# First projection columns taken by input rows, adaLN units moved, overflow list made at the end of expert 0

## The reference

```python
cond = silu(c)
for l in range(2):
    mod = cond @ ada_w[l] + ada_b[l]              # 6 x 1024: shift, scale, gate, twice
    sh_m, sc_m, g_m, sh_f, sc_f, g_f = split(mod, 6)
    h = rms_norm(x, mix_pre_g[l]) * (1 + sc_m) + sh_m
    z = h @ w_in[l]                                # 7696 columns
    y_a = conv branch(z): a*sigmoid(g), causal depthwise conv of 31 taps,
          layer norm, silu, @ w_conv_out
    y_b = stick-breaking attention of 8 heads @ w_sb_out
    y_c = gated linear attention of 4 heads (16 low-rank columns give its decay)
          @ w_gla_out
    y = (g_a*y_a + g_b*y_b + g_c*y_c) @ w_o        # sigmoid gates from z
    x = x + g_m * rms_norm(y, mix_post_g[l])
    h = rms_norm(x, ffn_pre_g[l]) * (1 + sc_f) + sh_f
    y = swiglu(h) if l == 0 else moe_swiglu(h)     # dense 2816; top 2 of 8 experts, 3584
    x = x + g_f * rms_norm(y, ffn_post_g[l])
```

## Time and profile before

| what | us |
|---|---|
| median of 3 runs | 1854.64 |
| lowest and highest | 1853.37 and 1854.91 |
| the profiled execution | 1851.58 |
| its span, first to last instruction | 1849.7 |
| TensorE matmul busy in the span | 1782.7 (96%) |
| VectorE busy | 1533.6 (83%) |
| ScalarE busy | 1133.5 (61%) |
| mean granted TensorE clock | 0.989 |

### The profile page before, as it was taken

How to read it: one execution, slowest core, us unless ns; L and a number is a source line. 1 busy time by engine, 2 the same in 40 slices (tenths; PEclk the granted TensorE clock), 3 DMA queues, 4 the chain that set the end, 5 groups by cost and what they waited for, 6 DMA issues and landing times.

```text
span 1849.7 us, 28685 instructions
## 1 busy us (share of the span) xinstructions
PE 1782.7 (96%) x10843; PEld 1577.2 (85%) x10844; DVE 1533.6 (83%) x1422; ACT 1133.5 (61%) x954; POOL 193.6 (10%) x159
## 2 busy tenths in 40 slices
PE   2999999999999999989999999999999999999997
PEld 2999999899979999978888888888888888888886
DVE  6998866999657667767889898898898988988986
ACT  3444564533354554656777777767777777677774
POOL 0396001000006900000000000000000000000000
PEclk7999999999999999999999999999999999999999
DMA  9865534699735333444999989989999899899992
GB/s 381 356 239 200 175 138 163 229 392 362 260 108 185 135 137 137 160 153 181 364 355 363 373 330 375 366 338 363 353 361 372 330 376 370 335 366 348 361 374 94
DMA packets 72521, 525.30 MB, mean 284 GB/s; under 512 B 8112, under 2 KB 8240, under 8 KB 8704
## 3 DMA queue, kind: packets, MB, share of 16 engines
q1 hardware_dynamic: 72288, 524.03, 74.6%
q0 software_dynamic: 160, 0.23, 0.0%
HBM read 523.17 MB, written 1.05 MB: 283 GB/s over the span
## 4 chain that ended last, share of the span: by engine, by line
PE 55%; DVE 2%; ACT 0%; issue 0%; DVEq 0%; ACTq 0%
PE bank L1654 33%; PE bank L1669 16%; PE bank L1689 2%; PE bank L1679 1%; PE bank L1381 1%; PE bank L1352 1%; PE bank L1709 0%; PE bank L1710 0%; DVE arena L943 0%; DVE arena L947 0%; PE bank L1619 0%; DVE arena L1066 0%; PE bank L1626 0%; DVE w_lo L878 0%; DVE arena L1058 0%
## 5 line engine op out<-in xcount | busy, mean ns | idle before, releaser
L1127 DVE TENSOR_TENSOR w_lo<-raw,w_hi 128x2048 fp32r<-128x2048 f32 x224 | 510.0, 2291 | 82.9 <-ACT w_hi L752 82.9
L752 ACT ACTIVATE w_hi<-raw 128x2048 fp32r<-128x2048 f32 x224 | 428.5, 1916 | 97.0 <-PE bank L1669 70.4
L1381 PE MATMUL bank<-acts,w_hi 128*128 128x256 f32 x2080 | 374.2, 284 | 27.7 <-DVE acts L933 21.1
L1381 PEld LDWEIGHTS bank<-acts,w_hi 128*128 128x128 f32 x2080 | 321.4, 191 | 33.1 <-issue 24.6
L1654 PE MATMUL bank<-acts 128*128 128x512 f32 x1248 | 304.3, 392 | 2.5 <-DVE acts L1127 2.5
L1654 PE MATMUL bank<-w_hi,acts 128*128 128x512 f32 x960 | 297.3, 391 | 0.0
L1381 PE MATMUL bank<-acts,w_lo 128*128 128x256 f32 x1040 | 292.6, 281 | 0.0
L1654 PEld LDWEIGHTS bank<-acts 128*128 128x128 f32 x1248 | 231.3, 188 | 49.3 <-DVE acts L1127 2.9
L1127 DVE TENSOR_TENSOR acts<-raw,acts 128x2048 fp32r<-128x2048 f32 x112 | 256.1, 2287 | 19.9 <-ACT acts L752 19.9
L752 ACT ACTIVATE acts<-raw 128x2048 fp32r<-128x2048 f32 x112 | 215.1, 1921 | 72.2 <-PE bank L1654 69.8
L1669 PE MATMUL bank<-w_hi,acts 128*128 128x512 f32 x832 | 256.1, 389 | 0.0
(11 more groups left out here) (234 smaller groups left out, 2120.7 us busy)
## 6 DMA issues: line engine op xcount, KB each, us to landing
raw<-in_experts SPq DMA_DIRECT2D x336, 1024.0 KB, 5.1
raw<-in_stream SPq DMA_DIRECT2D x161, 1024.0 KB, 6.3
arena<-in_x_t SPq DMA_DIRECT2D x1, 1024.0 KB, 11.8
out_t<-arena SPq DMA_DIRECT2D x2, 512.0 KB, 2.6
arena<-in_c_row SPq DMA_DIRECT2D x1, 512.0 KB, 4.7
arena<-in_vecs SPq DMA_DIRECT2D x1, 224.0 KB, 2.5
arena<-in_glr_w POOLq DMA_DIRECT2D x2, 64.0 KB, 4.2
arena<-in_a POOLq DMA_DIRECT2D x2, 32.0 KB, 4.5
```

The source lines that it names most:

```text
L752: act.activation(expert_hi[s], raw[:, slot, :], ACT.Copy).then_inc(hi_written, 1)
L1127: dve.tensor_tensor(expert_lo[s], raw[:, slot, :], f32(expert_hi[s]), ALU.subtract).then_inc(raw_taken, 1)
L1381: mm = pe.matmul(out[:, c, :], w[:, 256 * k + P * c:256 * k + P * c + P], (hi if high else lo)[:, k, :], start=(k == 0 and n == 0 and c == 0),
```

## The change

Four things are done together.

1. The first eight columns of layer 0's input projection (`FIRST`) come by input rows. A unit `("zk", 0, k, 0)` holds 128 rows of w_in, those of chunk k, by the 2048 columns of z 0 to 7. The stream begins ada 0, zk 0, ada 1, zk 1, and so on. As soon as ada k is taken, VectorE finishes chunk k of shift and scale, scales chunk k, takes the low part of zk k and splits the chunk; `project_rows` multiplies it into all eight banks at once. x is loaded first, in halves; five products on constants stand ahead of TensorE's first sums. The evacuation of the eight columns, the two `glu` and the low-rank product follow when all rows are in; conv taps of layer 0 run in the iterations 9 to 25, and on VectorE and GpSimd they wait for the low-rank product, which reads the same memory.
2. Of layer 0's other 16 adaLN units, five stand behind z columns 9, 11, 13, 15, 17, three behind 26, 27, 28, four behind the units of "wo", and four go first in the feed-forward. Units of g = 2 are laid out so that the first four hold the scale and the last four the gate.
3. `finish_mods` becomes four functions, each called where its values are first needed; `ADA_TURN` goes from (3, 6, 9) to (5, 7, 10).
4. `list_overflow` is called behind the last tile of expert 0.

```diff
+FIRST = 8
+ADA_AFTER = (9, 11, 13, 15, 17, 26, 27, 28)
 def plan():
-    units = [("ada", 0, 0, k) for k in range(KC)]
+    units = []
+    for k in range(KC):
+        units += [("ada", 0, 0, k), ("zk", 0, k, 0)]
     for layer in range(DEPTH):
-        later = [("ada", 0, g, k) for g in (1, 2) for k in range(KC)] if layer == 0 else []
-        for u in range(Z_UNITS + G_UNITS):
+        later = [("ada", 0, 1, k) for k in range(KC)] + [("ada", 0, 2, k) for k in range(4)]
+        for u in range(FIRST if layer == 0 else 0, Z_UNITS + G_UNITS):
             units.append(("z", layer, u, 0))
-            if later and (u < 9 or u % 2):
+            if layer == 0 and u in ADA_AFTER:
                 units.append(later.pop(0))
         units += [("out", layer, b, h) for b in (1, 0, 2) for h in range(2)]
-        units += [("wo", layer, q, 0) for q in range(4)]
+        for q in range(4):
+            units.append(("wo", layer, q, 0))
+            if layer == 0 and later:
+                units.append(later.pop(0))
         if layer == 0:
-            later = [("ada", 1, g, k) for g in range(3) for k in range(KC)]
+            later = [("ada", 0, 2, k) for k in range(4, KC)]
+            later += [("ada", 1, g, k) for g in range(3) for k in range(KC)]
...
 # SyncE
+            for half in range(2):
+                c = KC // 2 * half
+                sp.dma_start(x[:, c:c + KC // 2, :], x_t[:, c:c + KC // 2, :]).then_inc(x_loaded[half], 16)
+            sp.dma_start(cond[0], c_row.to_broadcast([P, D])).then_inc(cond_loaded, 16)
             sp.dma_start(ar[:, C_VEC:C_VEC + N_VEC], vecs).then_inc(vec_loaded, 16)
-            sp.dma_start(cond[0], c_row.to_broadcast([P, D])).then_inc(cond_loaded, 16)
             for n in range(RAW):
                 sp.dma_start(raw[:, n, :], stream[n]).then_inc(loaded[n], 16)
-                if n == 1:
-                    sp.dma_start(x, x_t).then_inc(x_loaded, 16)
...
 # GpSimd
                 wait_read(pool, ("z", layer, 3, 0))
+                pool.wait_ge(lr_ready, layer + 1)
                 taps(layer, 0, TAPS)
...
 # ScalarE
+            act.preload_act_table(ACT.Silu)
+            act.wait_ge(consts, 5)
+            square_x(0)
             act.wait_ge(cond_loaded, 16)
             act.activation(cond[0], cond[0], ACT.Silu).then_inc(cond_ready, 1)
             root_ahead()
-            act.wait_ge(consts, 5)
-            act.wait_ge(x_loaded, 16)
-            norm_x(0)
+            norm()
+            act.wait_ge(vec_loaded, 16)
+            write_hi(("zk", 0, 0, 0))
+            for k in range(KC):
+                shift_chunk(0, SH_M, 1, k)
+                if k + 1 < KC:
+                    write_hi(("zk", 0, k + 1, 0))
...
 # VectorE
+            dve.wait_ge(vec_loaded, 16)
+            for k in range(KC):
+                add_ada(next(order))
+                if k == 0:
+                    inverse_root()
+                finish_mixer_in(0, k)
+                scale_chunk(0, A_M, k)
+                take(("zk", 0, k, 0))
+                split_chunk(1, k)
...
-                        first = (4, 4, 6)[c]
+                        first = (4, 4, 6)[c] if layer else FIRST + 1
...
-                if layer == 0 and i == 12:
-                    finish_mods(0, 1)
-                if layer == 0 and i == 24:
-                    finish_mods(0, 2)
...
                         if i == 1:
+                            finish_mixer_out(0)
+                            finish_ffn_in(0)
                             mixer_out(layer)
...
                 add_result(step)
-                if first:
-                    list_overflow()
...
                         tile(step, r, q * 2, q * 2 + (1 + r), True)
+                if first:
+                    list_overflow()
                 column = column_of(step + 1)
                 select(column, sel, chosen_f, sel_ready)
...
 # TensorE
+            def project_rows(k):
+                u = ("zk", 0, k, 0)
+                pe.wait_ge(raw_taken, POS[u] + 1)
+                pe.wait_ge(h_split, k + 1)
+                s = SLOT[u]
+                for c in range(2 * FIRST):
+                    out = two(bank[c // 2])[:, c % 2, :]
+                    for n, (w, high) in enumerate(parts(s)):
+                        mm = pe.matmul(out, w[:, P * c:P * c + P], (h_hi if high else h_lo)[:, k, :],
+                                       start=(k == 0 and n == 0 and c % 2 == 0),
+                                       stop=(k == KC - 1 and n == 2), skip_group_check=True)
+                    if k == KC - 1 and c % 2 and c < 2 * FIRST - 1:
+                        mm.then_inc(columns_done, 1)
+                mm.then_inc(consumed, 1)
...
-                if i == 0:
+                if i == (0 if layer else FIRST):
+                    if layer == 0:
+                        wait_read(pe, ("z", layer, 7, 0))
                     low_rank(layer)
...
+            for _ in range(5):
+                pe.matmul(bank[0][:, :], ones, area(C_ID, 4 * P), start=True, stop=True)
             norm_sums()
+            pe.wait_ge(norm_root, 1)
+            for k in range(KC):
+                project_rows(k)
```

More of the change, by code:

```diff
@@ L102, in plan, with ada_groups @@
     return units
+def ada_groups(g, k):
+    if g == 2:
+        return [16 * g + 8 * (k // 4) + 2 * (k % 4) + j for j in range(2)]
+    return [16 * g + 8 * j + k for j in range(2)]
 PLAN = plan()
@@ L109 @@
 POS = {u: n for n, u in enumerate(PLAN)}
+ADA_EARLY = [u for u in PLAN if u[0] == "ada" and POS[u] < POS["z", 0, 27, 0]]
 WPOS = {u: n for n, u in enumerate(W_UNITS)}
@@ L373, in mixer_units @@
         def mixer_units(layer):
-            return [u for u in W_UNITS if u[1] == layer and u[0] in ("z", "out", "wo")]
+            first = [("z", 0, u, 0) for u in range(FIRST if layer == 0 else 0)]
+            return first + [u for u in W_UNITS if u[1] == layer and u[0] in ("z", "out", "wo")]
         def mixer_place(u):
             return mixer_units(u[1]).index(u)
-        BANKS = {}
-        used = [0] * 7
+        BANKS = {("z", 0, u, 0): [(u, 0)] for u in range(FIRST)}
+        used = [1] * 8
         turn_of = 0
-        for u in W_UNITS:
+        for u in W_UNITS[FIRST:]:
             if u[0] == "out" and mixer_place(u) % 3 != 1:
@@ L773, in _ @@
                         hook(layer, i)
+                    if layer == 0 and i == FIRST + 1:
+                        hook(layer, 2)
                 if layer == 0:
@@ L1580, in _ @@
                 for i, u in enumerate(mixer_units(layer)):
+                    if layer == 0 and i < FIRST:
+                        continue
                     if i == 0:
@@ L1782, in lay_out @@
         if kind == "ada":
[L1783 to L1784 removed]
+            stream[n] = np.concatenate([f["ada_w"][layer][:, P * m:P * m + P].T for m in ada_groups(a, b)], axis=1)
+        elif kind == "zk":
+            stream[n] = np.concatenate([f["w_in"][layer][P * a:P * a + P, cols[u][0]:cols[u][0] + 256]
+                                        for u in range(FIRST)], axis=1)
         elif kind == "z":
```

172 lines of the change are left out of this document (106 added, 66 removed).

## The result

The median of four runs is 1837.3 us (1835.7 to 1838.4) against 1854.0 for the kernel before (1852.0 to 1854.9): ratio 0.9912, 95% interval 0.9898 to 0.9926, 16.7 us faster. The forecast was 1835.1 with a range of 1827 to 1845. The profiled execution took 1838.4 us around a span of 1836.6, so between the two profiled spans there are 13.1 us; the sum of the prediction had 19.5. The total was met better than the terms were.

A forecast was written before the change was run, and what follows sets the result against it. TensorE, busy 96% of the span, sets the end once the first projection starts. Head 21.6, a removed wait 1.5, column 29 -1.8, second output unit -1.2, list -0.6: 19.5 off 1854.6 gives 1835.1 us, range 1827 to 1845.

The forecast's parts named there:

- The head: First eight columns by rows: VectorE sets 5.95 us a row, columns done at 66.3, gain 21.6 us (15.7 to 28.5).
- the rival: Rows: waits of some 0.3 us each hold TensorE at 1.2 GHz, columns end 39 us later, 1874 us; chance 0.05.
- The heads: Layer 0's heads: VectorE's average 8.4 us an iteration against TensorE's 8.4, a draw, with about 4 us of slack.
- The step that failed: Layer 0's conv taps in 17 iterations instead of 22, beside adaLN units: costed at nothing.
- The general bound: Cost of the conv taps and adaLN units in the heads: 0 to 8 us, one microsecond in each of eight heads.
- Column 29: The adaLN unit between columns 28 and 29 delays the low half TensorE needs: a loss of 1.8 us.
- the second output unit: An adaLN unit on VectorE ahead of this unit's low half, 1.11 of its 2.3 us in idle time: loss 1.2 us.
- The list: Overflow list of 3.5 us moved within expert 0: +2.6 at the start, -3.2 at the end, both together -0.6 us.
- the gap where the column's number is read: End of expert 0: next expert's column number read after the list, no longer hidden; 0.5 us more, bounds 0 and 1.5.

The follow-up runs named there:

- e4b: Changed kernel with five unused 512-column products on TensorE ahead of the first row; 1836.2 us.
- e9: e7 plus five unused products before the first row and two before each layer's first output projection; 1823.7 us.
- e2: Changed kernel with VectorE writing the gla states ahead of the conv taps in iteration 25 of each mixer layer; 1832.2 us.
- e8: Changed kernel with adaLN units in the old rhythm, behind columns 9, 11, 13 to 29, and one behind the first output unit; 1840.9 us.
- e6: Changed kernel with the adaLN unit before column 29 moved behind column 20, and the output projection's last one behind the third branch unit; 1835.9 us.
- e10: Changed kernel with the adaLN unit behind the first output unit moved behind the third branch unit; 1836.4 us.
- e3: Changed kernel with four unused 512-column products on TensorE before its wait for the gla states in iteration 25 of layer 0; 1835.4 us (one run).
- e5: Changed kernel with the overflow list's 17 operations spread over the second and third tile of expert 0; 1834.3 us.
- e7: Changed kernel with the edits of e2, e5 and e6 together; 1825.7 us.
- e1: Changed kernel with the overflow list back at its old place, the start of the first expert; 1836.9 us.

## Why the prediction came out as it did

**The head** was right, to 0.3 us at 66.3. Two errors met: VectorE's row is 5.74 us and not 5.95, which alone would give 1.5 less, and the first row's low clock is not used up "by the third or fourth row" but kept to the last, because 5.7 against 5.74 leaves no room to catch up. e4b shows what is behind that.

**The clock in the rows:** the rival had a chance of 0.05, and no row ran low after 24.5 us. In the changed kernel there was no test of it, as TensorE never waited; in e4b it had one gap of 0.2 us, in e9 three, and the clock stayed. Gaps of 0.3 in each row were not tried. So the rival was avoided by VectorE's faster rows and TensorE's late start, not refuted.

**The heads** were a draw, as costed: 22.91 us of lead at the first and at the last.

**The step that failed** is the one on the conv taps, "I cost it at nothing". It looked for the cost of 17 instead of 22 iterations, five and six taps each, only in the heads and at their softplus, and took the slack there. It did not go on to what VectorE does next for TensorE: the gla states at iteration 25. There the lead fell by 4.3 us: 1 of wait, and the rest, in the eight groups and the projection behind them, clock. e2 gave it back, and the older wait of 0.86 with it, by changing the order on VectorE alone. The general bound, 0 to 8 us for this stage, held it; the likeliest value did not. What e2 does not separate is how much of VectorE's lateness comes from the added taps per iteration and how much from TensorE's having lost a wait before; e8 shows that adaLN units there would add 2.9 us of wait.

**Column 29** (-1.8) measured -1.67, **the second output unit** (-1.2) measured -1.1; e6 and e10 show that the units are the cause, and that about 1.0 of the wait at the latter stays when the unit goes. The prediction counted only the wait. In the changed kernel's profile the clock stayed at 1.00 behind it; in e2, e3, e5, e7 and e9 it did not, which cost another 1.6.

**The list:** at the start +2.85 for +2.6. At the end the term of -3.2 was mis-sized: -5.4. Its parts are the list, 3.3 us instead of 3.5; the gap where the column's number is read, 1.23 us exposed instead of 0.5, inside the bound of 1.5; and in four of the eight kernels with this list (the changed one, e6, e8, e10) another 1.6 us of low clock over the last down products. The move as a whole is -1.0 or -2.6 instead of -0.6.

**The sum.** The profiled spans give 22.9 - 4.3 - 1.7 - 1.1 - 0.1 (layer 1) - 2.6 (the list) - 0.1 (the end) = 13.0, against 19.5. The medians give 16.7. The kernel before had been profiled in an execution 2.4 us faster than its median, the changed one in one 1.0 slower. That the forecast lies 2.2 us from the median is in part this luck.

## What to carry to other kernels

When a helper engine's work is packed into fewer iterations, follow it past the stage under study to the next thing that the main engine waits for from it; the order of two jobs inside one iteration may be worth more than their number. Small serial jobs such as the list cost all of their time at a stage boundary and nothing if they are dealt out over a steady stage in which that engine idles. And a wait of about 2 us on TensorE should be entered with two prices, itself and a possible stretch at the low clock behind it. The second is not paid where another engine holds TensorE up right behind, as between the first two output units here.

## What was unexpected of the hardware

A wait of the same length does not always bring the low clock. The wait of 1.86 us before the last down product of expert 0 was followed by twelve products in 4.60 us in the changed kernel and in 3.03 in e2:

```profile
944.33 3.03 PE L1784 MATMUL bank<-acts 128*128 128x512 f32 x12 [1.86 <-DVE acts L1351]
```

Likewise at the second output unit: the wait of 2.09 us left the grant at 1.00 in the changed kernel, while the same wait in e2 was followed by three microseconds at half clock.

```profile
281.43 0.50 PE L1470 MATMUL bank<-acts,w_hi 128*128 128x256 f32 x2 [2.09 <-DVE w_lo L929]
```
```profile
282.00:285.00 3.00, 3.00 (x17) 3.00 (x16) 3.00 (x5) 1.95 (x3) 0.00 (x0) 0.51 1.00 391
```

At the first output unit the clock fell behind a wait of 2.3 in e1 and e4b, and not behind one of 2.30 in e2; where it fell there, nothing was lost, as VectorE's low half of the next unit sets the start (8.8 us later in either case). At iteration 25 the clock fell behind each of the seven waits of 1.9 to 2.1 and behind the one of 4.8, and not behind 0.86. Which of two outcomes a wait has is worth up to 2.8 us in this kernel; what decides was not settled. The other surprise was the gap of 1.23 us on VectorE where a number is read into a register with nothing to hide it.
